# A hybrid SSD / attention / expert block: the four late modulation rows made in the projection stage instead of the attention stage

## The chip, the cores and the metric

One core of one Trainium2 chip runs the whole kernel in one launch. The metric is the device time of that launch in microseconds (us); the median of three runs is 2930.75 us (2930.63 to 2934.76).

## The reference, cut to what matters

One trunk layer over 1024 latent tokens of width 1024, all in float32:

```python
mod = jax.nn.silu(c) @ w_ada[l] + b_ada[l]                 # 1 x 6144
sh1, sc1, g1, sh2, sc2, g2 = [m[:, None, :] for m in jnp.split(mod, 6, axis=-1)]
h = modulate(layer_norm(x), sh1, sc1)
y, yc = token_mixer(h, hc, cos, sin, w_in[l], ...)         # projection, SSD scan, attention, gates, w_o
x = layer_norm_affine(DEEPNORM_ALPHA * x + g1 * y, ln1_g[l], ln1_b[l])
h = modulate(layer_norm(x), sh2, sc2)
x = layer_norm_affine(DEEPNORM_ALPHA * x + g2 * expert_choice_ffn(h, ...), ln2_g[l], ln2_b[l])
```

The first two rows of `mod` (sh1, sc1) are needed at the very start and are made there. The case is about the other four, g1, sh2, sc2 and g2: each is a product of the 1024 numbers silu(c) with a 1024 x 1024 part of `w_ada`, plus a part of `b_ada`. They are first used after the output projection `w_o`.

## The kernel before, in words

The program is a sequence of stages; each is a block in which every engine has its own instruction stream, and a block ends with all engines meeting. The stages are: front (norm, first modulation), projection of features (`project_f_stage`), projection of tokens with the state recurrence (`project_states_stage`), scan output, attention, branch, residual, experts, output.

**`project_f_stage`** makes 24 channel blocks of xBC, 10 of q and k, and 16 gate blocks, each of 128 output features by 1024 tokens. For one block SyncE loads 512 KB of `w_in` (L368), ScalarE and VectorE split it in a high and a low part (L447, L522), TensorE makes 48 matmuls (L386), and ScalarE takes the result out of PSUM (L479 for a gate, with a sigmoid). GpSimd stores the results: `store_split` (L599, L601) the q and k blocks, `store` (L593) the gates. TensorE goes through gates 2 to 15 in a hardware loop. While gates are made, the buffers `qk_hi`, `qk_lo`, `conv_acc` and `t_out`, and the PSUM bank `f_tp`, are unused. `Ahead` is the first weight slab of the next stage, loaded and split here (L511, L569).

**`attention_stage`** goes through 8 query blocks of 128 tokens. A table of tiles sets the order: 20 tiles for a middle query block, each with a score product (L1498), an exponential (L1549) and a product with the values (L1510); row maxima for the next block (L1482, L1579) lie between. SyncE does the small transfers between engines for every block: `gather_sums` (L1418), `spread_inverse` (L1423, then a wait, then L1428), `load_top` (L1406 to L1410), and the query loads (L1395 to L1397). Beside this GpSimd makes the four modulation rows. `w_ada` is split so that partition p holds rows 8p to 8p+7, so a row needs 8 parts of [128, 1024] (512 KB each), 32 in all:

```python
pool.dma_start(ada_w[:, j % RING], wa[:, k, (2 + c) * D:(3 + c) * D])          # L1653, load_part
G_.tensor_scalar(ada_w[..], ada_w[..], ada_cond[:, k:k + 1], None, ALU.mult)   # L1663, scale
G_.tensor_tensor(ada_sum[..], ada_sum[..], ada_w[..], ALU.add)                 # L1666, add
```

The sum over the 128 partitions is left undone there; each of the four [128, 1024] sums goes to DRAM as `mod_parts` (L1682).

**`residual_stage`** multiplies by `w_o`, which it loads in four slabs of 1 MB through two buffers (L1953) and splits (ScalarE L2120, VectorE L2206). Before its first product TensorE spreads seven rows over all partitions (`spread_row`, L2028 and L2030): the three plain rows b_o, ln1_g and ln1_b by a matmul that picks one of seven, and the four modulation rows by this and a matmul of `ones` with the 2 MB of `mod_parts` (L2117), which adds up the partitions. ScalarE keeps them (`keep_row`, L2109 and L2111) between its casts of the weight slabs, and stores g2 for the expert stage. TensorE's first product with `w_o` (L2001) needs all seven rows spread and all four slabs split.

Of the kernel before, what the change touches and what calls it, by code (L numbers as in the profile page):

```python
# [15 lines left out]
ALU = mybir.AluOpType  # L16
ACT = mybir.ActivationFunctionType
AX_X = mybir.AxisListType.X
F32 = mybir.dt.float32
# [4 lines left out]
P = 128  # L24
D = 1024
KT = D // P
# [274 lines left out]
def project_f_stage(s, hi, lo, ahead, xbcF, xbcT, qkH, qkL, gF):  # L301
# [7 lines left out]
    with ExitStack() as st:  # L309
# [12 lines left out]
        tap = own(st, nc, "conv_tap_cols", [P, 2, CONV_W + 1])  # L322
        lat = bank(st, nc, "f_lat", [P, 2, SEQ])
# [12 lines left out]
        ctx_turned = s.sem("f_ctx_turned")  # L336
        rot_step = s.sem("f_rot_step")
# [7 lines left out]
        NF = NX + NQK + NG  # L345

# [9 lines left out]
        with nc.Block() as block:  # L356

            @block.sync
            def _(sp):
# [4 lines left out]
                for col, f0, n in ((XBC0, 0, NX), (Q0, NX, NQK), (G0, NX + NQK, NG)):  # L364
                    with sp.Fori(0, n // 2) as i:
                        for b in range(2):
                            sp.wait_ge(w_free, 2 * i + (f0 + b + 1))
                            sp.dma_start(w[:, b], wv[:, :, ds(2 * P * i + (col + P * b), P)]).then_inc(w_in[b], 16)  # L368
                ahead.load(s, sp)

            @block.tensor
            def _(pe):
# [60 lines left out]
                with pe.Fori(1, NG // 2) as i:  # L433
                    for b in range(2):
                        product(2 * i + (NX + NQK + b), b, False)

            @block.scalar
            def _(act):
# [16 lines left out]
                def evacuate(f, b, kind, turn, within):  # L455
# [20 lines left out]
                    else:  # L476
                        act.wait_ge(qk_lo_made, NQK - 1 + b)
                        act.wait_ge(wide_out[b], 16 * turn - 16 * NQK // 2)
# [36 lines left out]
            def _(dve):  # L515
# [49 lines left out]
                with dve.Fori(1, NG // 2) as i:  # L565
                    split_lo(2 * i + (NX + NQK), 0)
                    split_lo(2 * i + (NX + NQK + 1), 1)
                dve.wait_ge(ahead.hi_made, 1)
                nc.vector.tensor_tensor(ahead.lo[:], ahead.raw[:], ahead.hi[:].bitcast(F32), ALU.subtract).then_inc(ahead.split, 1)  # L569

            @block.gpsimd
            def _(pool):
# [9 lines left out]
                def store(f, b, kind, turn, within):  # L582
                    row = within * P
                    rows = slice(row, row + P) if isinstance(row, int) else ds(row, P)
                    if kind == "xbc":
                        pool.wait_ge(wide_made, f + 3)
                        pool.dma_start(xbcF[rows, :], wide[:, b]).then_inc(wide_out[b], 16)
                        pool.wait_ge(tp_free, f + 2)
                        pool.dma_start(xbcT[:, rows].rearrange("(c p) n -> p c n", p=P),
                                       turned[:, b].rearrange("p (c n) -> p c n", n=P)).then_inc(turned_out[b], 16)  # L590
                    else:
                        pool.wait_ge(acc_free, f + 3)
# [2163 lines left out]
```

## Time and profile before

| what | value |
| --- | --- |
| median of 3 runs | 2930.75 us |
| the profiled execution: its own time, and its span from first to last instruction | 2933.16 us, 2931.5 us |
| TensorE busy / GpSimd busy over the span | 2504.5 us (85%) / 705.8 us (24%) |
| granted TensorE clock, mean | 0.915 of full |
| gates in `project_f_stage` | from about 628 to 797 us |
| attention stage | from about 1314 to 1680 us |
| residual stage | from 2047.9 us, first product with `w_o` at 2103.6 us |

A profile row tells for a group of instructions the line, engine, operation, output<-input by the program's names, the count, the busy time and the mean of one, and the idle time of the engine before them with what ended it. PE is TensorE, DVE VectorE, ACT ScalarE, POOL GpSimd, SP SyncE; PEld is TensorE's weight load, and a q behind an engine's name its instruction queue. Times of a row in the timeline are start and duration in us.

### The profile page before, as it was taken

To read this page: it belongs to the slowest core of one execution; us is meant where nothing else is said; L and a number is where in the kernel's file an instruction comes from. 1 tells how busy PE (TensorE), PEld (TensorE's weight loads), DVE (VectorE), ACT (ScalarE), POOL (GpSimd) and SP (SyncE) were. 2 spreads that over 40 slices of the span, in tenths; PEclk is the share of its full clock that TensorE was granted. 3 is DMA by queue.
4 is the path that set the end of the run, shared out by engine and by line. 5 is a ranking of instruction groups with operands and counts; after the bars stand their busy time and mean duration, and the time that the engine had idled before them with its cause. 6 is when DMAs were issued, how large, how long until landed. Compare 5 with 4: busy or idle time off the path is not lost. (4 is left out here: it accounts for less than half of the span.)

```text
span 2931.5 us, 31293 instructions
## 1 busy us (share of the span) xinstructions
PE 2504.5 (85%) x11848; PEld 1972.9 (67%) x11848; DVE 1597.0 (54%) x1674; ACT 1061.7 (36%) x1349; POOL 705.8 (24%) x487
## 2 busy tenths in 40 slices
PE   6799999999898996975989659698885499999992
PEld 2588888778697885653656448576474388888881
DVE  4455554431143665763556352532254699999994
ACT  3333333121131113541334341310232377777772
POOL 0001000010002434994992000000042212222113
PEclk8799999999999998996999869899697699999996
DMA  4333333342225867949564255543333599999994
GB/s 188 97 109 116 117 117 108 115 144 86 89 88 197 299 241 247 308 164 202 148 157 88 54 167 150 161 118 94 119 115 113 222 375 397 391 395 398 398 362 143
DMA packets 307553, 556.80 MB, mean 190 GB/s; under 512 B 22121, under 2 KB 212025, under 8 KB 283953
## 3 DMA queue, kind: packets, MB, share of 16 engines
q1 hardware_dynamic: 277938, 431.61, 43.3%
q0 software_dynamic: 27200, 115.10, 12.1%
q10 hardware_dynamic: 2304, 8.62, 0.8%
q8 instruction: 68, 1.11, 0.2%
q14 instruction: 43, 0.35, 0.0%
HBM read 434.22 MB, written 120.79 MB: 189 GB/s over the span
## 5 line engine op out<-in xcount | busy, mean ns | idle before, releaser
L2412 DVE TENSOR_TENSOR e_wlo<-e_w,e_whi 128x2048 fp32r<-128x2048 f32 x188 | 425.7, 2290 | 43.5 <-ACT e_whi L2365 42.2
L2365 ACT CAST e_whi<-e_w 128x2048 fp32r<-128x2048 f32 x192 | 366.3, 1915 | 120.8 <-PE e_gu L2525 83.5
L386 PE MATMUL f_lat<-h_hi,w_hi 128*128 128x512 f32 x800 | 254.4, 399 | 0.3 <-DVE w_lo L522 0.3
L386 PE MATMUL f_lat<-h_lo,w_hi 128*128 128x512 f32 x800 | 250.7, 394 | 0.0
L386 PE MATMUL f_lat<-h_hi,w_lo 128*128 128x512 f32 x800 | 250.6, 394 | 0.0
L522 DVE TENSOR_TENSOR w_lo<-w_raw,w_hi 128x1024 fp32r<-128x1024 f32 x50 | 61.3, 1225 | 216.9 <-ACT w_hi L447 216.9
L1889 PE MATMUL b_acc<-b_hi,b_whi 128*128 128x512 f32 x384 | 151.4, 394 | 14.0 <-DVE b_lo L1840 14.0
L1579 DVE CUSTOM_DVE_ANT_0 a_masked<-a_a_ps,a_mask 128x640 f32<-128x640 f32 x128 | 105.5, 825 | 99.3 <-PE a_a_ps L1483 95.9
L1510 PE MATMUL a_c_ps<-a_prob,a_v 128*128 128x512 f32 x304 | 157.8, 602 | 0.0
L386 PEld LDWEIGHTS f_lat<-h_hi,w_hi 128*128 128x128 f32 x800 | 136.0, 188 | 30.5 <-issue 4.8
L386 PEld LDWEIGHTS f_lat<-h_hi,w_lo 128*128 128x128 f32 x800 | 136.0, 188 | 27.7
L386 PEld LDWEIGHTS f_lat<-h_lo,w_hi 128*128 128x128 f32 x800 | 136.0, 188 | 27.5
L1549 ACT ACTIVATE a_prob<-a_b_ps 128x512 f32<-128x512 f32 x152 | 89.5, 597 | 177.4 <-DVE a_b_ps L1597 84.5
L535 DVE SCALAR_TENSOR_TENSOR conv_acc<-conv_in,conv_tap_cols,conv_acc 128x1284 f32<-128x1284 f32 x96 | 149.4, 1556 | 3.4
L1889 PE MATMUL b_acc<-b_lo,b_whi 128*128 128x512 f32 x384 | 151.1, 393 | 0.0
L1889 PE MATMUL b_acc<-b_hi,b_wlo 128*128 128x512 f32 x384 | 150.7, 393 | 0.0
L2525 PE MATMUL e_gu<-e_whi,e_xhi 128*128 128x512 f32 x512 | 140.4, 396 | 3.9 <-DVE e_xlo L2416 2.4
L2525 PE MATMUL e_gu<-e_wlo,e_xhi 128*128 128x512 f32 x512 | 138.6, 393 | 0.0
L2525 PE MATMUL e_gu<-e_whi,e_xlo 128*128 128x512 f32 x512 | 138.6, 393 | 0.0
L1498 PE MATMUL a_b_ps<-a_q,a_k 128*128 128x512 f32 x152 | 120.9, 796 | 18.9 <-ACT a_prob L1549 10.7
L2589 POOL DMA_INDIRECT moe<-e_y,e_scatter_rows x16 | 44.6, 2785 | 378.0 <-DVE e_y L2433 378.0
L1482 PE MATMUL a_a_ps<-a_k,a_q 128*128 128x256 f32 (+1 forms) x256 | 80.8, 335 | 44.5 <-DMA a_q<-qkH 41.1
(346 smaller groups left out, 5627.8 us busy)
## 6 DMA issues: line engine op xcount, KB each, us to landing
e_w<-in_w_gate_up SPq DMA_DIRECT2D x128, 1024.0 KB, 10.4
e_w<-in_w_down SPq DMA_DIRECT2D x64, 1024.0 KB, 8.7
w_raw<-in_w_in SPq DMA_DIRECT2D x50, 512.0 KB, 4.0
t_space<-xbcT POOLq DMA_DIRECT2D x18, 1280.0 KB, 6.4
before<-t_space SPq DMA_DIRECT2D x16, 1024.0 KB, 4.2
y_before<-before SPq DMA_DIRECT2D x64, 256.0 KB, 6.1
a_ada_w<-in_w_ada POOLq DMA_DIRECT2D x32, 512.0 KB, 4.1
b_w<-in_w_ssd_br SPq DMA_DIRECT2D x16, 1024.0 KB, 5.6
```

Of the source, the lines that this page charges most:

```text
L386: mm = nc.tensor.matmul(o, weights[:, b, k, :], part[:, k, a:a + n], start=(k == 0 and n_pass == 0), stop=(k == KT - 1 and n_pass == 2))
L522: nc.vector.tensor_tensor(wlo[:, b], w[:, b], whi[:, b].bitcast(F32), ALU.subtract).then_inc(w_free, 1)
L535: nc.vector.scalar_tensor_tensor(conv[:, b], padded[:, b, c:c + W_OUT], tap[:, b, c:c + 1], conv[:, b], ALU.mult, ALU.add).then_inc(conv_s ...
L1482: nc.tensor.matmul(a_ps[:, h % 2, out], q1[:, j, h], k1[:, g, keys], start=True, stop=False)
L1498: nc.tensor.matmul(b_ps[:, T % 2], k1[:, g, keys], q1[:, n % QB, heads], start=True, stop=False)
L1510: nc.tensor.matmul(out, values(v, c, g), prob[:, T % PR], start=first, stop=last).then_inc(tiles_summed, 1)
L1549: nc.scalar.activation(prob[:, T % PR], b_ps[:, T % 2], ACT.Exp, scale=SCALE).then_inc(exps_made, 1)
L1579: V.tensor_tensor_reduce(masked[:, h % 2], a_ps[:, h % 2, A0:A0 + KEYS], mask[:, variant(m)], 1.0, NEG, ALU.add, ALU.max, top[:, h:h + 1]) ...
L1889: mm = nc.tensor.matmul(acc[:, b, j], weights[:, b, k, :], xpart[:, k, :], start=(k == ks[0] and n_pass == 0), stop=(k == ks[-1] and n_pas ...
L2365: nc.scalar.copy(whi[:, slot % SPLIT], w[:, slot]).then_inc(w_hi, 1)
L2412: V.tensor_tensor(wlo[:, slot % SPLIT], w[:, slot], whi[:, slot % SPLIT].bitcast(F32), ALU.subtract).then_inc(w_split, 1)
L2525: mm = nc.tensor.matmul(gu[:, 512 * c:512 * c + 512], part[:, b, k, :], weights[:, slot % SPLIT, 512 * c:512 * c + 512], start=(k == 0 and ...
```

## The change

The four rows are made in `project_f_stage`, by GpSimd, while TensorE makes the gates. The 32 parts go the same way (load, scale, add), now with 8 adds for each row onto a sum that is cleared first and holds the bias in partition 0. TensorE sums the 128 partitions by a matmul with a column of ones: rows 0, 1 and 2 after gates 5, 9 and 13, and row 3 after the last gate. VectorE copies a row out of PSUM, and SyncE stores it to `mod`. GpSimd's gate stores go to SyncE, on the queue of the weight loads, and the gate loops are written out. In the attention stage nothing is left of this work. In the residual stage the seven spread rows are gone: six rows are loaded from DRAM with a broadcast over the partitions, by ScalarE behind its first cast, and the `mF` tile 1 is loaded before slab 2. The core of the diff:

```diff
 def project_f_stage
+        ada_w = (qhi[:, 0, 0:D].bitcast(F32), qhi[:, 1, 0:D].bitcast(F32), qlo[:, 0, 0:D].bitcast(F32))
+        ada_sum, ada_row = (conv[:, 0, 0:D], conv[:, 1, 0:D]), turned[0:1, 0, 0:D]
+        SUM_AFTER = {5: 0, 9: 1, 13: 2}
@@ sync
+                for n in range(NG):
+                    sp.wait_ge(w_free, NX + NQK + n + 1)
+                    sp.dma_start(w[:, n % 2], wv[:, :, G0 + P * n:G0 + P * n + P]).then_inc(w_in[n % 2], 16)
+                    if n >= 3:
+                        store_gate(n - 3)
+                    if n - 2 in SUM_AFTER:
+                        store_rest(SUM_AFTER[n - 2])
                 ahead.load(s, sp)
...
@@ tensor
-                with pe.Fori(1, NG // 2) as i:
-                    for b in range(2):
-                        product(2 * i + (NX + NQK + b), b, False)
+                def sum_rest(c):
+                    pe.wait_ge(ada_step, KT * c + KT)
...
+                    for half in range(2):
+                        mm = nc.tensor.matmul(tp[0:1, 512 * half:512 * half + 512], ones[:], ada_sum[c % 2][:, 512 * half:512 * half + 512], start=True, stop=True)
+                    mm.then_inc(ada_summed, 1)
+                for n in range(2, NG):
+                    product(NX + NQK + n, n % 2, False)
+                    if n in SUM_AFTER:
+                        sum_rest(SUM_AFTER[n])
+                sum_rest(REST - 1)
@@ vector
+                def keep_row(c):
+                    dve.wait_ge(ada_summed, c + 1)
+                    if c:
+                        dve.wait_ge(ada_out, 16 * c)
+                    nc.vector.tensor_copy(ada_row, tp[0:1, :]).then_inc(ada_made, 1)
...
@@ gpsimd
-                pairs(pool, "gate", store)
+                def load_part(j):
+                    c, k = divmod(j, KT)
+                    if j >= 3:
+                        pool.wait_ge(ada_step, j - 2)
+                    pool.dma_start(ada_w[j % 3], wa[:, k, (2 + c) * D:(3 + c) * D]).then_inc(ada_in[j % 3], 16)
...
+                for b in range(2):
+                    pool.wait_ge(qk_out[b], 16 * (NQK + NQK - NQ))
+                    pool.wait_ge(turned_out[b], 16 * NX // 2 + 16)
+                pool.wait_ge(rot_step, 2 * NQK)
+                pool.wait_ge(cond_in, 16)
+                clear_sum(0)
+                for j in range(2):
+                    load_part(j)
+                for j in range(PARTS):
+                    if j + 2 < PARTS:
+                        load_part(j + 2)
+                    if j % KT == 4 and j // KT + 1 < REST:
+                        clear_sum(j // KT + 1)
+                    add_part(j)
+                pool.wait_ge(ada_out, 16 * REST)
 def attention_stage
...
-                for j in range(PARTS):
-                    if j + RING - 1 < PARTS:
-                        load_part(j + RING - 1)
-                    add_part(j)
...
 def residual_stage
@@ sync
                 load_w(1)
+                load_m(1)
                 for n in range(2, 4):
                     sp.wait_ge(w_split, n - 1)
                     load_w(n)
-                load_m(1)
@@ tensor
-                for j in range(len(ROWS)):
-                    spread_row(j)
                 pe.wait_ge(w_split, 4)
@@ scalar
-                    if n >= 1:
-                        keep_row(2 * n - 2)
-                        keep_row(2 * n - 1)
+                    if n == 0:
+                        for j, row in ((G1, mod[0:1, 2 * D:3 * D]), (B_O, s.x["b_o"]), (LN_G, s.x["ln1_g"]), (LN_B, s.x["ln1_b"]),
+                                       (SC2, mod[0:1, 4 * D:5 * D]), (SH2, mod[0:1, 3 * D:4 * D])):
+                            act.dma_start(rowv[:, j], row.to_broadcast([P, D])).then_inc(rows_in, 16)
```

How GpSimd's stream stands behind the last q and k store (`qk_lo`) in `project_f_stage`; before, the gate stores alone, in a loop:

```order
L601 DMA qkL<-qk_lo 128x256
L352 UNCONDITIONAL_BRANCH
L352 ISA
L593 ISA
L593 DMA gF<-f_out 128x1024
L592 REGISTER_ALU
L593 ISA
L593 DMA gF<-f_out 128x1024
L352 REGISTER_ALU
L352 COMPARE_AND_BRANCH
L593 DMA gF<-f_out 128x1024 x2
L356 UNCONDITIONAL_BRANCH
```

and now (the parts of `w_ada` lie in `qk_hi` and `qk_lo`, the sum in `conv_acc`):

```order
L660 DMA qkL<-qk_lo 128x256
L675 MEMSET conv_acc 128x1024
L677 DMA conv_acc<-in_b_ada 1x16x64
L670 DMA qk_hi<-in_w_ada 128x1024 x2
L670 DMA qk_lo<-in_w_ada 128x1024
L682 ISA
L682 TENSOR_SCALAR qk_hi<-qk_hi,f_cond 128x1024
L687 TENSOR_TENSOR conv_acc<-conv_acc,qk_hi 128x1024
L670 DMA qk_hi<-in_w_ada 128x1024
L682 TENSOR_SCALAR qk_hi<-qk_hi,f_cond 128x1024
L687 TENSOR_TENSOR conv_acc<-conv_acc,qk_hi 128x1024
```

The last three rows repeat to the 32nd part, with a clear and a bias load before parts 4, 12 and 20; no gate store is left there.

TensorE's stream at the end of the gates and into the next stage (`t_acc`), now:

```order
L421 MATMUL f_lat<-h_lo,w_hi 128x512 x2
L421 MATMUL f_lat<-h_hi,w_lo 128x512 x2
L477 MATMUL f_tp<-conv_acc,f_ones 1x512 x2
L367 UNCONDITIONAL_BRANCH
L869 UNCONDITIONAL_BRANCH
L877 MATMUL t_acc<-t_w_first_hi,h_hi 128x320
```

The L477 row is new; it stands between the last gate and the branch out of the block, and likewise behind gates 5, 9 and 13.

ScalarE's stream from the start of the residual stage to its last weight cast, now:

```order
L2134 CAST r_whi<-r_w 128x8x256
L2138 DMA r_rows<-mod 128x1024
L2138 DMA r_rows<-in_b_o 128x1024
L2138 DMA r_rows<-in_ln_g 128x1024
L2138 DMA r_rows<-in_ln_b 128x1024
L2138 DMA r_rows<-mod 128x1024 x2
L2092 CAST r_mhi<-r_m 128x1024
L2134 CAST r_whi<-r_w 128x8x256
L2092 CAST r_mhi<-r_m 128x1024
L2134 CAST r_whi<-r_w 128x8x256 x2
```

Before, six copies of spread rows (L2111) stood between these casts, two behind each of the last three, and a seventh (L2109) behind them.

## Rows read from the trace of the kernel before

**Rows 1.** The page: the head, and the group of VectorE's weight splits.
```profile
span 2931.5 us, 31293 instructions
...
L522 DVE TENSOR_TENSOR w_lo<-w_raw,w_hi 128x1024 fp32r<-128x1024 f32 x50 | 61.3, 1225 | 216.9 <-ACT w_hi L447 216.9
```

**Rows 2.** Timeline, gates and the start of the next stage: start, duration, what [idle before].
```profile
640.81 0.55 POOL L601 DMA_DIRECT2D qkL<-qk_lo  x1
...
786.10 1.02 ACT L479 ACTIVATE f_out<-f_lat 128x1024 f32<-128x1024 f32 x1 [9.24 <-PE f_lat L386]
...
797.30 1.02 ACT L479 ACTIVATE f_out<-f_lat 128x1024 f32<-128x1024 f32 x1 [7.96 <-PE f_lat L386]
798.62 0.53 POOL L593 DMA_DIRECT2D gF<-f_out  x1 [10.67 <-ACT f_out L479]
...
806.15 0.31 POOL L970 MEMSET t_zeros<- 128x256 f32 x1 [6.99 <-POOLq L356]
```

**Rows 3.** Timeline of GpSimd in the attention stage, one part and the next one's start.
```profile
1428.74 2.85 POOL L1663 TENSOR_SCALAR a_ada_w<-a_ada_w,a_ada_cond 128x1024 f32<-128x1024 f32 x1
1431.67 2.35 POOL L1666 TENSOR_TENSOR a_ada_sum<-a_ada_sum,a_ada_w 128x1024 f32<-128x1024 f32 x1
1434.32 0.59 POOL L1653 DMA_DIRECT2D a_ada_w<-in_w_ada  x1 [0.30 <-POOL a_ada_sum L1666]
1434.96 2.84 POOL L1663 TENSOR_SCALAR a_ada_w<-a_ada_w,a_ada_cond 128x1024 f32<-128x1024 f32 x1
```

**Rows 4.** Timeline of SyncE's queue, attention: the same step of blocks 0, 3, 4.
```profile
1414.21 0.56 SPq L1418 DMA_DIRECT2D a_sums<-a_cols  x1
...
1539.61 0.54 SPq L1418 DMA_DIRECT2D a_sums<-a_cols  x1
...
1575.51 0.55 SPq L1418 DMA_DIRECT2D a_sums<-a_cols  x1
```

**Rows 5.** Windows, attention: us, PE PEld DVE ACT POOL busy, clock, DMA share, GB/s.
```profile
1355.00:1375.00 20.00, 6.44 (x20) 4.77 (x20) 4.17 (x10) 0.00 (x0) 11.91 (x10) 0.60 1.05 226
1400.00:1555.00 155.00, 143.42 (x560) 96.30 (x559) 89.93 (x181) 54.69 (x98) 143.71 (x76) 0.96 0.62 157
1555.00:1655.00 100.00, 100.00 (x379) 64.92 (x378) 53.91 (x116) 44.21 (x80) 0.35 (x1) 1.00 0.26 55
```

**Rows 6.** Timeline of TensorE at the start of attention.
```profile
1362.83 0.58 PE L1482 MATMUL a_a_ps<-a_k,a_q 128*128 128x256 f32 x1 [9.72 <-DMA a_q<-qkH]
...
1377.49 0.80 PE L1498 MATMUL a_b_ps<-a_q,a_k 128*128 128x512 f32 x1 [8.14 <-DMA a_sunk_spread<-a_sunk]
```

**Rows 7.** Windows, start of the residual stage; columns as in rows 5.
```profile
2050.00:2066.00 16.00, 3.79 (x5) 1.73 (x6) 3.64 (x3) 4.84 (x4) 0.00 (x0) 0.50 1.02 354
```

**Rows 8.** Timeline at the start of the residual stage: ScalarE, TensorE, VectorE.
```profile
2053.61 1.90 ACT L2120 CAST r_whi<-r_w 128x2048 fp32r<-128x2048 f32 x1 [42.45 <-DMA r_w<-in_w_o]
...
2062.21 3.75 PE L2028 MATMUL r_row_ps<-r_base_rows,r_ident 7*128 7x512 f32 x4 [21.29 <-DMA r_parts<-mod_parts]
...
2092.58 2.29 DVE L2206 TENSOR_TENSOR r_wlo<-r_w,r_whi 128x2048 fp32r<-128x2048 f32 x1 [12.30 <-ACT r_whi L2120]
...
2103.56 1.84 PE L2001 MATMUL r_acc<-r_whi,r_mhi 128*128 128x512 f32 x2
```

**Rows 9.** DMA issues: count, KB each, median us from issue to landing.
```profile
qkL<-qk_lo POOLq DMA_DIRECT2D x2, 128.0 KB, 4.9
...
a_ada_w<-in_w_ada POOLq DMA_DIRECT2D x32, 512.0 KB, 4.1
```

**Rows 10.** Timeline, VectorE and GpSimd at once: states stage, then attention stage.
```profile
970.42 3.63 POOL L968 TENSOR_TENSOR t_space<-t_space,t_tab 128x2048 f32<-128x2048 f32 x1
...
971.85 4.37 DVE L898 TENSOR_TENSOR t_space<-t_space,t_tab 128x2048 f32<-128x2048 f32 x1
...
998.89 4.00 POOL L968 TENSOR_TENSOR t_space<-t_space,t_tab 128x2048 f32<-128x2048 f32 x1 [0.93 <-DMA t_space<-xbcT]
...
1437.15 0.67 DVE L1611 TENSOR_TENSOR a_cols<-a_cols,a_inverse 64x512 f32<-64x512 f32 x1
```

More of the change, by code:

```diff
@@ L336, in project_f_stage @@
         ctx_turned = s.sem("f_ctx_turned")
+        cond_in, ones_made, ada_in = s.sem("f_cond_in"), s.sem("f_ones_made"), [s.sem(f"f_ada_in{b}") for b in range(3)]
+        gate_out = [s.sem(f"f_gate_out{b}") for b in range(2)]
+        ada_blank, ada_bias_in = s.sem("f_ada_blank"), s.sem("f_ada_bias_in")
+        ada_scaled, ada_step, ada_summed, ada_made, ada_out = (s.sem(f"f_ada_{n}") for n in ("scaled", "step", "summed", "made", "out"))
         rot_step = s.sem("f_rot_step")
@@ L345, in project_f_stage @@
         NF = NX + NQK + NG
+        REST = 4
+        PARTS = REST * KT
+        SUM_AFTER = {5: 0, 9: 1, 13: 2}
+        wa = s.x["w_ada"][0].rearrange("(p k) n -> p k n", k=KT)
         def pairs(eng, kind, step):
@@ L1325, in attention_stage @@
         sums, inv_sums = own(st, nc, "a_sums", [P, QH]), own(st, nc, "a_inv_sums", [P, QH])
-        RING = 3
-        PARTS = 4 * KT
-        ada_cond, ada_w, ada_sum = own(st, nc, "a_ada_cond", [P, KT]), own(st, nc, "a_ada_w", [P, RING, D]), own(st, nc, "a_ada_sum", [P, 2, D])
-        cond_in, ada_in = s.sem("a_cond_in"), [s.sem(f"a_ada_in{b}") for b in range(RING)]
-        ada_scaled, ada_step, ada_out = s.sem("a_ada_scaled"), s.sem("a_ada_step"), [s.sem(f"a_ada_out{b}") for b in range(2)]
-        wa = s.x["w_ada"][0].rearrange("(p k) n -> p k n", k=KT)
         a_ps = bank(st, nc, "a_a_ps", [P, 2, 1024])
@@ L2102, in keep_turned @@
                     nc.scalar.copy(h2F[:], tp[:]).then_inc(cols_made, 1)
-                def keep_row(j):
-                    kind = ROWS[j][0]
-                    out = (row_ps[:], tp[:].rearrange("p k q -> p (k q)"))[j % 2]
-                    act.wait_ge(spread, j + 1)
-                    if kind is None:
-                        nc.scalar.copy(g2[:], out[0:1]).then_inc(rows_kept, 1)
-                    else:
-                        nc.scalar.copy(rowv[:, kind], out).then_inc(rows_kept, 1)
-                act.dma_start(ident[:], s.squares[:, 0:P]).then_inc(const_in, 16)
-                for j, (kind, part) in enumerate(ROWS):
-                    src = s.x["b_ada"][:, (2 + part) * D:(3 + part) * D] if part is not None else s.x[{B_O: "b_o", LN_G: "ln1_g", LN_B: "ln1_b"}[kind]]
-                    act.dma_start(base_rows[j:j + 1, :], src).then_inc(base_in, 16)
-                act.dma_start(parts[:], mod_parts).then_inc(parts_in, 16)
                 for n in range(4):
```

156 lines of the change are left out of this document (67 added, 89 removed).

## The prediction, made before the changed kernel ran

> **What bounds the kernel now.** I read the page first, for the busy share of each engine, and then the timeline of each of the three stages that the change touches, since each has a limit of its own. The chain that ended last covers only the output stage and says nothing here.
>
> In the gates TensorE is the bound. The sigmoid copies of two gates that follow each other start 11.20 us apart (786.10 and 797.30), and every gate from the second on keeps that pace; GpSimd only issues a store for each, and the next stage starts 7.5 us after the last store's issue [rows 2]. VectorE has one split of 1.2 us in each 11.2 us [rows 1]. So GpSimd has the time from 640.8 to about 797 us nearly free, some 156 us.
>
> The work that is to go there takes longer. In the attention stage one part costs GpSimd 6.22 us from scale to scale: 2.85 scale, 2.35 add, then 0.30 and 0.59 for the issue of the next load, and small gaps [rows 3]. GpSimd waits for hardly anything else there; it is a chain on one engine, and 32 parts make 199 us. **32 times 6.22 does not fit in 156.**
>
> In attention this work is off the chain of computing but not free. SyncE's step `gather_sums` comes once in a block of 20 tiles. Blocks 0 to 3 take 125.4 us for three (41.8 each) while the loads of `w_ada` run, and the next, after the last load, 35.9 us [rows 4]. The windows say the same: up to 1555 us TensorE is busy 143.4 of 155 us at clock 0.96 with the DMA engines at 0.62; after it, busy all the time at 1.00, DMA at 0.26 [rows 5]. The parts compete with the query loads and the small round trips on which a block's start hangs. At the start of the stage the DMA engines are full from 1355 to 1375 us (226 GB/s), and TensorE waits 9.7 us for queries and 8.1 us for a small transfer behind them [rows 5, 6].
>
> In the residual stage the first product starts at 2103.6 us, though the first slab was in at 2053.6 [rows 8]. Between them TensorE spreads seven rows at a granted clock of 0.50 [rows 7], after the 2 MB of `mod_parts` have landed at 2062.2, and ScalarE's row copies hold up its cast of the last slab, so that this slab's split starts only at 2092.6 [rows 8].
>
> **The change, part by part.**
>
> 1. *The rows in the gates.* GpSimd's last q/k store is issued at 640.8 and lands 4.9 us later [rows 2, 9]: 645.7. The clear of 1024 columns: 0.31 us for 256 [rows 2], so at most 1.2. Then 0.3 and 0.55 us until the bias load is issued, 4.1 us for the first part to land [rows 9] and 0.3 to start: 652.2. Thirty parts at 6.22: 838.8. The last two have no load to issue, 5.3 each: 849.4. Three more clears with their bias loads at 1.2 + 0.3 + 0.55 = 2.05: 855.6.
>
> TensorE cannot run ahead of this. After gate 5 (end about 685) it waits for part 8, due at 652.2 + 49.8 + 2.05 = 704, so 19 us; after gate 9 and gate 13 a few us each; gate 15 ends at about 832, and then it waits some 25 us for part 32. None of these waits adds to the end: GpSimd never waits for TensorE (the clears that need a sum come 20 us behind it), so the end is GpSimd's. What is queued behind the waiting TensorE, VectorE's split and row copy and SyncE's loads, is two gates ahead and has slack. I cost the moved gate stores, the written-out loops and the three inner sums (at most 3.75 us each) at nothing: GpSimd's chain covers them by some 25 us, and without that cover the sums would cost 8 to 11 us.
>
> Then the tail, which nothing covers: four matmul instructions at half clock, 3.75 us [rows 8], VectorE's copy of 1024 columns, half of the 2.29 us for 2048 [rows 8], and a store up to the next stage, for which I take the 7.5 us of the gate store. Together 12.4.
>
> 2. *Sharing with VectorE.* In the states stage a VectorE operation on two SBUF operands that starts inside one of GpSimd's takes 4.37 us; it ends 2.17 us after GpSimd's ends, which is its bare length. GpSimd's own went from 3.63 to 4.00 us beside such an operation [rows 10]. So each holds the other up. But a VectorE operation at 1437.15 took a bare 0.67 us inside GpSimd's scale of 1434.96 to 1437.80 [rows 3, 10]: the scale lets go long before its end. About 13 splits of 1.2 us fall in the chain. One that meets an add waits for its end and runs in the 0.9 us before the next scale, at 0.3 us for GpSimd; one in the first half of a scale costs nothing. I take 0.3 us each, 4 us in all, between 0 and 13 x 1.2 = 16.
>
> The Trainium skill ("SBUF — State Buffer", section "SBUF: two separate sides") speaks against this change: whichever of VectorE and GpSimd starts first has the shared pair of ports for its whole instruction, and the other is blocked. The states rows agree; the 0.67 us inside the scale does not. By the rule alone the sum would have 16 us here and not 4.
>
> So the stage ends at 855.6 + 4 + 12.4 = 872.0 and not at 806.15: **65.9 us later.**
>
> 3. *Attention without the parts.* Three blocks fall from 41.8 to 35.9 us: 17.7 us. At the start, four loads of 0.5 MB fall into the full queue, 2.1 MB, 9.3 us at 226 GB/s; TensorE's two waits there total 17.9 us. Not all of a queue's time is on the chain, so I take 6, between 0 and 9.3. **23.7 us earlier**, between 17.7 and 27. GpSimd's own time of 190 us that goes is worth nothing: it ended 100 us before the stage.
>
> 4. *Residual stage.* Seven spreads on TensorE, seven copies on ScalarE and 2 MB go; six broadcasts of 512 KB come. The first product now waits for the last slab alone. Bytes until it is in: 4 MB of weights, 1 MB of `mF`, 3 MB of rows, 8.4 million bytes; at the 354 GB/s from 2050 on [rows 7], that is 23.7 us, then 1.90 cast and 2.29 split: 2077.9. **25.7 us earlier** than 2103.6. With the 226 GB/s of the attention start it would be 37.2 us of loading, and 12.2 earlier; with the row loads out of the way, 14.8 us of loading and 34.6 earlier. I take 354, the rate of the same loads in the same place. The rows' own wait (VectorE before the first norm) is covered by the first product of 13 us.
>
> Sum: 65.9 - 23.7 - 25.7 = +16.5 us on a span of 2931.5: 2948.0. The profiled execution's own time is 1.7 above its span and 2.4 above the median of the runs, so against the median of 2930.75 this is **2947 us**.
>
> **The rivals.**
>
> *A. The port lock in full* (the rule above): every split in the chain costs GpSimd its 1.2 us, 16 and not 4. 2959 us. For it, the states rows; against it, the operation inside the scale. Chance 0.12.
>
> *B. The broadcasts crowd out the slabs.* The residual stage gains 12.2 us and not 25.7, as at 226 GB/s: 2961 us. For it, a queue of small pieces does run at that rate in attention; against it, the row loads here have long pieces of 4 KB. Chance 0.10.
>
> *C. The giving back is at its upper ends*, 27 and 34.6 us: +4.3, 2935 us, within what can be told from no change, about 0.2% or 5.9 us. For it, the start of attention is all transfers; against it, the slabs go through two buffers, each waiting for a split. Chance 0.14.
>
> *D. Faster: GpSimd's part is shorter here.* If the load's issue and its wait (0.9 us) fell out of the chain, because the queue now has this work alone, a part would take 5.3 us, the chain would be 28 us shorter and the 4 us of sharing gone too: 65.9 - 32 - 49.4 = -15, about 2915 us. It decides from 5.5 us a part down. Against it: the wait comes before every issue, full queue or not [rows 3], and the code's order of load, scale and add is the same. Chance 0.07.
>
> **How the numbers follow.** The forecast of 2947 has the remaining 0.57, between about 2939 and 2955. Slower by over 0.2%: the forecast, A and B, less a little, 0.77. Within 0.2%: nearly all of C and that little, 0.15. Faster: D and the edge of C, 0.08. The range from 2934 to 2962 takes in A, B and C alone; it leaves out D and A with B together.
>
> **What would show it.** The next stage starting near 872 us. GpSimd busy without a break from 646 to 858, at 6.2 us a part. TensorE waiting about 19 us for GpSimd after gate 5 and 25 us after the last gate. `gather_sums` 36 us apart in all middle blocks. In the residual stage, the first product some 30 us after the stage's start and not 56. I am wrong if GpSimd's part takes below 5.5 us, if TensorE has no wait after gate 5, or if the attention blocks stay above 40 us without the loads.

## The result, and the profile after

The changed kernel takes 2953.5 us (median of 4 runs, 2949.7 to 2956.7) beside 2932.8 for the kernel before in the same session: ratio 1.0068, 95% interval [1.0048, 1.0089]. A second comparison of the unaltered change, with more runs, gave 2951.1 beside 2934.0: 1.0064 [1.0051, 1.0076]. **It is 17 to 21 us slower.** The profiled execution of the change took 2949.7 us, the fastest of its four, with a span of 2948.2; that is 16.7 more than the span of 2931.5 before.

The timeline of GpSimd, VectorE, TensorE and SyncE in the changed kernel, at the start of the gates, at gate 5, at gate 9 and at the end of the stage (start us, duration us, engine, line, operation, out<-in; in brackets the idle time before and what ended it). The last row but one is the first instruction of the next stage and answers to the last one of [rows 2]:

```profile
641.07 0.55 POOL L660 DMA_DIRECT2D qkL<-qk_lo  x1
647.75 0.95 POOL L675 MEMSET conv_acc<- 128x1024 f32 x1 [6.13 <-issue]
653.73 2.85 POOL L682 TENSOR_SCALAR qk_hi<-qk_hi,f_cond 128x1024 f32<-128x1024 f32 x1 [2.62 <-DMA qk_hi<-in_w_ada]
656.66 2.39 POOL L687 TENSOR_TENSOR conv_acc<-conv_acc,qk_hi 128x1024 f32<-128x1024 f32 x1
659.35 0.60 POOL L670 DMA_DIRECT2D qk_hi<-in_w_ada  x1 [0.30 <-POOL conv_acc L687]
660.00 2.85 POOL L682 TENSOR_SCALAR qk_hi<-qk_hi,f_cond 128x1024 f32<-128x1024 f32 x1
...
704.55 3.17 PE L477 MATMUL f_tp<-conv_acc,f_ones 128*1 128x512 f32 x4 [19.09 <-POOL conv_acc L687]
...
761.63 1.21 DVE L623 COPY t_out<-f_tp 1x1024 f32<-1x1024 f32 x1 [15.07 <-PE f_tp L477]
761.83 4.39 POOL L687 TENSOR_TENSOR conv_acc<-conv_acc,qk_hi 128x1024 f32<-128x1024 f32 x1
762.77 1.20 DVE L575 TENSOR_TENSOR w_lo<-w_raw,w_hi 128x1024 fp32r<-128x1024 f32 x1
...
860.92 2.34 POOL L687 TENSOR_TENSOR conv_acc<-conv_acc,qk_hi 128x1024 f32<-128x1024 f32 x1
863.31 3.57 PE L477 MATMUL f_tp<-conv_acc,f_ones 128*1 128x512 f32 x4 [24.84 <-POOL conv_acc L687]
866.92 1.21 DVE L623 COPY t_out<-f_tp 1x1024 f32<-1x1024 f32 x1 [31.70 <-PE f_tp L477]
868.16 0.25 SPq L389 DMA_DIRECT2D mod<-t_out  x1
875.41 0.31 POOL L1066 MEMSET t_zeros<- 128x256 f32 x1 [12.15 <-POOLq L367]
```

The first part takes 6.27 us from scale to scale (653.73 to 660.00); the parts that nothing disturbs take 6.20 to 6.28. The chain takes 209.5 us from the first scale to the end of the last add at 863.3, and the next stage starts 12.15 us later, at 875.4. Before it was 806.15: 69.3 us. TensorE waited 19.1 us at its first sum and 24.8 at its last, and once the chain ran nothing held GpSimd up except VectorE's operations at the same time (the add of 4.39 us). The groups of GpSimd's operations over the whole chain (mean ns behind the busy time) give the sum of that: 174.6 us for 32 scales and 32 adds, which at their bare 2.85 and 2.34 would be 166.1, so 8.5 us of sharing (10.5 us in the trace of x11, the same kernel run again):

```profile
L682 POOL TENSOR_SCALAR qk_hi<-qk_hi,f_cond 128x1024 f32<-128x1024 f32 x22 | 64.4, 2926 | 3.5 <-DMA qk_hi<-in_w_ada 2.6
L687 POOL TENSOR_TENSOR conv_acc<-conv_acc,qk_hi 128x1024 f32<-128x1024 f32 x22 | 56.3, 2558 | 1.8
L682 POOL TENSOR_SCALAR qk_lo<-qk_lo,f_cond 128x1024 f32<-128x1024 f32 x10 | 28.5, 2854 | 0.4
L687 POOL TENSOR_TENSOR conv_acc<-conv_acc,qk_lo 128x1024 f32<-128x1024 f32 x10 | 25.4, 2540 | 0.8
```

From there two stages give back. In attention, `gather_sums` (L1508 now) of the blocks that took 41.8 us each [rows 4]:

```profile
1473.76 0.56 SPq L1508 DMA_DIRECT2D a_sums<-a_cols  x1
...
1509.81 0.55 SPq L1508 DMA_DIRECT2D a_sums<-a_cols  x1
...
1581.65 0.54 SPq L1508 DMA_DIRECT2D a_sums<-a_cols  x1
```

That is 36.0 us a block, 107.9 for three and not 125.4. In the residual stage the row copies are gone from ScalarE, and the splits of the four slabs (before, the last of them came at 2092.6 [rows 8]) are these, with the wait of TensorE behind them:

```profile
2096.25 2.29 DVE L2213 TENSOR_TENSOR r_wlo<-r_w,r_whi 128x2048 fp32r<-128x2048 f32 x1 [11.98 <-ACT r_whi L2134]
2101.02 2.29 DVE L2213 TENSOR_TENSOR r_wlo<-r_w,r_whi 128x2048 fp32r<-128x2048 f32 x1 [1.34 <-ACT r_whi L2134]
2114.87 2.29 DVE L2213 TENSOR_TENSOR r_wlo<-r_w,r_whi 128x2048 fp32r<-128x2048 f32 x1 [2.47 <-ACT r_whi L2134]
2117.86 2.29 DVE L2213 TENSOR_TENSOR r_wlo<-r_w,r_whi 128x2048 fp32r<-128x2048 f32 x1 [0.70 <-ACT r_whi L2134]
```
```profile
PE r_acc L2049 <- DVE r_wlo L2213: 38.0, 1, 38.0
```

The first product starts at 2120.2. The stage began at 2089.2, so 31.0 us after the start and not 55.6. The balance, each as the shift against the kernel before at the marks named: gates +69.3 (next stage's start, 806.1 to 875.4); states and scan +2.1 (attention's first matmul, 1332.2 to 1403.6, is 71.4 later); attention -29.5 (the branch stage's first transpose, 1692.5 to 1734.4, is 41.9 later); branch -0.6; residual -24.6 (first product 16.7 later). The rest moves by nothing: the span is 16.7 longer. This is the balance of one trace against one; how far single terms of it scatter is said below the next table.

### The profile page after: what moved, and what is told of

The parts are those of the page before. It is cut to its first block and busy times, and to the rows that moved or that the text cites. A ratio compares the mean times of both kernels' runs of the same rounds, so it can differ in the third digit from the quotient of the medians.

```text
span 2948.2 us, 31069 instructions
## 1 busy us (share of the span) xinstructions
PE 2468.5 (84%) x11820; PEld 1957.5 (66%) x11820; DVE 1598.5 (54%) x1678; ACT 1054.9 (36%) x1342; POOL 711.7 (24%) x478
```

## The experiments

All are compared with the kernel before in their own session; where a run is set against the change, the change's 2951.1 us of its longer comparison (x11) is used. Three marks are read from every trace: the start of the stage after the gates, the length of attention (first matmul on queries and keys to the branch stage's first transpose), and the time from the residual stage's first cast to its first product.

| run | median us | ratio to before [95%] | gates end | attention | residual |
|---|---|---|---|---|---|
| before | | | 806.1 | 360.4 | 50.0 |
| change | 2953.5 | 1.0068 [1.0048, 1.0089] | 875.4 | 330.9 | 25.9 |
| x1 gate stores alone | 2929.5 | 0.998 [0.997, 0.999] | 805.7 | 353.6 | 49.2 |
| x2 24 parts (work left out) | 2901.6 | 0.9885 [0.9864, 0.9906] | 825.9 | 330.4 | 26.1 |
| x3 16 parts (work left out) | 2891.1 | 0.9845 [0.9823, 0.9868] | 814.9 | 330.9 | 25.7 |
| x4 sums last | 2949.7 | 1.0046 [1.0029, 1.0063] | 874.0 | 330.9 | 26.0 |
| x5 loads in attention | 2966.7 | 1.0113 [1.0096, 1.0129] | 877.1 | 351.4 | 25.7 |
| x6 compute in attention | 2960.3 | 1.0094 [1.0077, 1.0110] | 878.3 | 336.8 | 25.8 |
| x7 parts on VectorE | 2891.4 | 0.9864 [0.9847, 0.9880] | 815.6 | 331.1 | 25.8 |
| x8 rows late | 2947.1 | 1.0044 [1.0030, 1.0058] | 880.3 | 332.4 | 18.9 |
| x9 = x7 + x8 | 2886.7 | 0.9837 [0.9819, 0.9855] | 816.8 | 331.3 | 18.8 |
| x10 splits twice | 2958.0 | 1.0076 [1.0056, 1.0096] | 888.4 | 331.1 | 25.7 |
| x11 change again | 2951.1 | 1.0064 [1.0051, 1.0076] | 878.0 | 331.0 | 25.6 |
| x12 both in attention | 2975.0 | 1.0144 [1.0129, 1.0158] | 878.2 | 355.5 | 25.5 |

How close a single trace may be read shows where several have the same code. The gates of the change stand in six traces (change, x5, x6, x8, x11, x12) and end at 875.4 to 880.3 us, the change's own being the earliest. Its attention stands in nine and takes 330.4 to 332.4. The attention of the kernel before stands in two, and takes 360.4 in its own trace and 353.6 in x1. The kernel before has medians of 2932.4 to 2935.2 in the sessions, so a difference of medians from two sessions is good to some 3 us.

### What sets the end of the gates

**x1**: the kernel before, with the gate loops written out and the stores on SyncE.

```diff
-                        pool.wait_ge(acc_free, f + 3)
-                        pool.dma_start(gF[rows, :], wide[:, b, CTX:TOK]).then_inc(wide_out[b], 16)
+                    sp.wait_ge(acc_free, f + 3)
+                    sp.dma_start(gF[row:row + P, :], wide[:, n % 2, CTX:TOK]).then_inc(gate_out[n % 2], 16)
```

> Only one part of the change is made: the gate loops written out and the gate stores issued by SyncE; the modulation rows stay in attention and the residual stage is the old one. Theory 1 (the added time is GpSimd's chain of 32 parts and nothing else in the gates): the gates end where they did, 806 us within 2 us, and the time is that of the kernel before, 2931 us, within 3 us. Rival (part of the 69 us comes from the stores behind SyncE's weight loads, or from the written-out loops): the gates end 5 us or more later, the time is 2936 us or more. A small gain of 3 to 5 us at the gates' end would also be possible, since the last store no longer goes through GpSimd.

Measured: the gates end at 805.7 us against 806.1, and the time is 0.1 to 0.3% under the kernel before. The stores and the loops cost nothing, as the prediction had them. The small gain is not in the gates; in this trace it lies in attention (353.6 us, with the same code there), and I do not know why. Its three blocks took 121.5 us where the trace before had 125.4:

```profile
1409.05 0.56 SPq L1431 DMA_DIRECT2D a_sums<-a_cols  x1
...
1530.56 0.54 SPq L1431 DMA_DIRECT2D a_sums<-a_cols  x1
```

So what the change gives back in attention is 22.7 to 29.5 us, by which of the two traces it is set against.

**x2** and **x3**: fewer parts, all else as in the change. Each of the four rows is summed from six, or four, of its eight parts, so these two kernels leave out work of the reference and are no versions of it; they serve as a measure alone.

```diff
+        NK = 6
-        PARTS = REST * KT
+        PARTS = REST * NK
```

> The change with 24 parts in place of 32: each row is summed from six of its eight parts, and the last two loads, scales and adds of each row are left out; sums, copies and stores stay. Theory 1 (GpSimd's chain sets the end of the gates): 8 parts of 6.27 us fall from the end, 50 us, and a microsecond or two of port sharing: the chain ends at about 812 us, the stage at about 824, the whole at 2901 us (2897 to 2906). Rival (TensorE's waits for sums and the clock that falls in them make the end): three inner sums and their waits stay, the end moves by less than 30 us and the time stays above 2920.

> The same with 16 parts, half of each row left out. The chain would end at about 762 us, before TensorE's last gate at 798. Theory 1: GpSimd no longer sets the end; TensorE does, with three inner sums of up to 3.75 us each on its path and the tail after the last gate (sum, copy, store), so the stage ends at 806 plus 8 to 15 us, 814 to 821, and the time is 2891 to 2899 us, only a few us under the run with 24 parts. Rival (every part costs its 6.27 us wherever it lies, for instance by crowding the weight loads): another 50 us less than with 24 parts, about 2850 us.

Measured: 8 parts fewer end the gates 49.5 us earlier (875.4 to 825.9), 6.2 us each, and the time falls by as much, to 2901.6. Sixteen fewer end them only 11.0 us earlier again, at 814.9. So down to some 22 parts (an estimate: 60.5 us of gain at 6.2 us each is about 10 parts) each costs its full length, and below that TensorE sets the end. The waits in the gates show the change of hands: in x3 it is GpSimd that waits for TensorE's sum to clear a sum buffer (first row), in the change TensorE for GpSimd (second row, all four sums; us in total, times, longest):

```profile
POOL conv_acc L676 <- PE f_tp L478: 13.5, 1, 13.5
```
```profile
PE f_tp L477 <- POOL conv_acc L687: 54.3, 4, 24.8
```

What is left is 814.9 against 806.1, 8.8 us. Each of the three inner sums lengthens its gate from 11.3 to 13.3 us (by the starts of the sigmoid copies), 6.1 us in all; the rest, 2.7 us, is put down to the last sum with its copy and store, and is within the scatter above.

**x4**: all four sums behind the last gate, from four buffers.

```diff
-        SUM_AFTER = {5: 0, 9: 1, 13: 2}
+        SUM_AFTER = {15: 0}
-                    if n in SUM_AFTER:
-                        sum_rest(SUM_AFTER[n])
-                sum_rest(REST - 1)
+                for c in range(REST):
+                    sum_rest(c)
```

> The change with all four column sums behind the last gate, from four separate sum buffers; the work is all there. TensorE then runs its 16 gates without waiting for GpSimd, and VectorE's splits come 11.2 us apart as before. Theory 1: GpSimd's chain is still the end, so it ends within 5 us of 863 us; behind it only the last sum, copy and store remain, the same 12 us: 2950 us within 5. Rival (the waits of TensorE on the inner sums cost the time, and the clock that falls meanwhile): the end of the gates comes back by 20 us or more, 2930 us or less.

Measured: TensorE now waits for GpSimd behind its last gate alone, 55.1 us in two pieces, the longer 44.3 (54.3 in the change, in four pieces), and the gates end at 874.0. Where it waits is without effect on the end; the rival falls.

**x10**: 14 more VectorE operations beside GpSimd's chain.

```diff
                 for n in range(2, NG):
+                    dve.wait_ge(hi_made, NX + NQK + n + 1)
+                    dve.wait_ge(extra, n - 2)
+                    nc.vector.tensor_tensor(padded[:, 0, 0:D], w[:, n % 2].rearrange("p k n -> p (k n)"), whi[:, n % 2].bitcast(F32).rearrange("p k n -> p (k n)"), ALU.subtract).then_inc(extra, 1)
                     split_lo(NX + NQK + n, n % 2)
```

> The changed kernel with 14 more VectorE operations in the gates: before each split the same subtraction of 1024 columns once more, into a buffer that nobody reads. It does no work of the reference, and TensorE doesn't need it. Theory 1 (GpSimd's chain lets most VectorE operations by, at 0.3 to 0.5 us each): the chain ends 4 to 7 us later than 863 us, 2955 to 2961 us. Rival A (the port is held in full for each): 14 times 1.2 us, 17 us later, 2967 us or more. Rival B (VectorE finds its gaps at no cost): 2951 us.

Measured by the groups of the chain in this trace:

```profile
L686 POOL TENSOR_SCALAR qk_hi<-qk_hi,f_cond 128x1024 f32<-128x1024 f32 x22 | 62.8, 2854 | 5.4 <-DMA qk_hi<-in_w_ada 4.5
L691 POOL TENSOR_TENSOR conv_acc<-conv_acc,qk_hi 128x1024 f32<-128x1024 f32 x22 | 61.3, 2785 | 1.8
L686 POOL TENSOR_SCALAR qk_lo<-qk_lo,f_cond 128x1024 f32<-128x1024 f32 x10 | 30.0, 2996 | 0.4
L691 POOL TENSOR_TENSOR conv_acc<-conv_acc,qk_lo 128x1024 f32<-128x1024 f32 x10 | 29.5, 2948 | 0.8
```

183.6 us, 9.0 more than in the change's first trace and 7.0 more than in its second (176.6): 0.5 to 0.64 us for each added operation, where the lock in full was priced at 1.2. The chain's end missed what Theory 1 expected: it ends at 876.2, 13 us later than the change's 863.3, and not 4 to 7. Of this, 4 us are a later start (the first scale at 657.7), which has nothing to do with the chain, and 9.0 are its sharing. The median, 2958.0, lies within what Theory 1 expected and under the 2967 of the full lock; whether the price is 0.5 or 0.64 it cannot tell.

### What attention gave back

**x5**: the 32 loads alone; **x6**: the scales and adds alone; **x12**: both, tied together as before.

```diff
+                for j in range(4 * KT):
+                    if j:
+                        pool.wait_ge(ada_in, 16 * j)
+                    pool.dma_start(ada_w[:, j % 3], wa[:, j % KT, (2 + j // KT) * D:(3 + j // KT) * D]).then_inc(ada_in, 16)
```
```diff
+                for j in range(4 * KT):
+                    if j:
+                        pool.wait_ge(ada_step, j)
+                    G_.tensor_scalar(ada_w[:, j % 3], ada_w[:, j % 3], 0.5, None, ALU.mult).then_inc(ada_scaled, 1)
+                    pool.wait_ge(ada_scaled, j + 1)
+                    G_.tensor_tensor(ada_sum[:], ada_sum[:], ada_w[:, j % 3], ALU.add).then_inc(ada_step, 1)
```

> The changed kernel, and in attention the 32 loads of w_ada (512 KB each) once more, one behind the other, into a buffer that nobody reads; no scale or add. They do no work of the reference. Theory 1 (attention gained because these transfers went): the blocks with loads go back to 40 to 42 us from 36, for as long as the loads run (32 at 5 to 6 us, 160 to 190 us, four blocks or so), and the start loses its gain too: 20 to 30 us slower than the change, 2970 to 2982 us. Rival (GpSimd's scale and add held VectorE up at the shared port): the blocks stay at 36 us, 2951 us within 4.

> The changed kernel, and in attention GpSimd's 32 scales and adds of 1024 columns once more, on a cleared buffer and without any load; they do no work of the reference. Theory 1 (it was the transfers): blocks at 36 to 37 us, 2951 us, at most 5 us more. Rival (port sharing): the blocks at 40 us or more while the chain of 32 x 5.2 us runs, 2965 us or more.

> The changed kernel, with both the 32 loads and the 32 scales and adds once more in attention, tied together as they were in the kernel before; they do no work of the reference. Loads alone made the attention stage 20.6 us longer in the trace, compute alone 6.0 us, and the kernel before is 29.5 us longer. If the two add up, with the residual stage as in the change: the stage 27 to 30 us longer, 2976 to 2982 us. If they hide behind each other, 20 us or less, 2971 us.

Measured: against the change, the loads alone cost 15.6 us in the medians (2966.7 - 2951.1), the compute alone 9.2, both together 23.9. In the traces attention grows by 20.5, 5.9 and 24.6 us. Neither theory had it whole: **the transfers are the larger part, between three fifths (by the medians) and three quarters (by the traces), and GpSimd's computing is the rest**, and the two nearly add up. Together they bring attention back to 355.5 us, between the two traces that have the old code (353.6 and 360.4). The medians expected for x5 (2970 and more) were missed by 3 us, for x6 (2956 at most) by 4, for x12 (2976 and more) by 1, and the stage in x12 grew by 24.6 us where 27 to 30 were expected.

Each has its own marks. With the loads, VectorE waits for the round trip of `inv_rows`, once in a block (an 8 KB store and a load of 512 KB that spreads it). These are its two transfers in x5 and then in the change, with the median us from issue to landing behind the size:

```profile
a_inverse<-inv_rows SPq DMA_DIRECT2D x3, 512.0 KB, 6.7
inv_rows<-a_inv_sums SPq DMA_DIRECT2D x3, 8.0 KB, 3.8
```
```profile
a_inverse<-inv_rows SPq DMA_DIRECT2D x4, 512.0 KB, 4.7
inv_rows<-a_inv_sums SPq DMA_DIRECT2D x4, 8.0 KB, 1.4
```

The round trip is 4.4 us longer beside the loads, and the blocks are 4.1 to 5.1 us longer; beside the computing (x6) it takes 1.4 and 4.9. TensorE's waits for ScalarE's exponentials from 1440 to 1600 us total 8.4 us in x5, 3.4 in x6 and none in the change. That these waits follow from the round trip was not traced step by step. With the computing, VectorE's short operations on SBUF operands grow. The groups and a wait, x5 first, then x6, then the change, all from 1400 (the wait from 1440) to 1600 us:

```profile
DVE a_cols L1704 <- DMA a_inverse<-inv_rows: 9.4, 3, 3.6
```
```profile
L1704 DVE TENSOR_TENSOR a_cols<-a_cols,a_inverse 64x512 f32<-64x512 f32 x12 | 7.9, 675 | 9.4 <-DMA a_inverse<-inv_rows 9.4
```
```profile
L1703 DVE TENSOR_TENSOR a_cols<-a_cols,a_inverse 64x512 f32<-64x512 f32 x12 | 14.2, 1199 | 1.4 <-DMA a_inverse<-inv_rows 1.4
L1694 DVE TENSOR_TENSOR a_sums<-a_sums,a_sunk_spread 128x16 f32<-128x16 f32 x4 | 7.7, 1928 | 0.0
```
```profile
L1701 DVE TENSOR_TENSOR a_cols<-a_cols,a_inverse 64x512 f32<-64x512 f32 x12 | 7.9, 674 | 0.1
L1692 DVE TENSOR_TENSOR a_sums<-a_sums,a_sunk_spread 128x16 f32<-128x16 f32 x4 | 0.7, 170 | 0.0
```

The division of columns takes 675 ns in the change and beside the loads, 1199 beside the computing; the sums' add 170 and 1928. The blocks of x6 are 37.3 to 38.2 us apart, those of x5 40.1 to 41.1, those of the change 36.0.

### What the residual stage gave back

**x8**: the six broadcasts behind ScalarE's last cast.

```diff
-                    if n == 0:
+                    if n == 3:
                         for j, row in ((G1, mod[0:1, 2 * D:3 * D]), (B_O, s.x["b_o"]), (LN_G, s.x["ln1_g"]), (LN_B, s.x["ln1_b"]),
```

> The changed kernel with the six row broadcasts of the residual stage issued after ScalarE's cast of the last slab and not after that of the first, so that the slabs have the queues for themselves. Theory 1: the 3 MB of rows stood in the way of the slabs (9 us at 340 GB/s), so the first product comes 7 to 10 us earlier; of this some goes back, since the rows then land behind the first product of 13 us and the first norm waits: 2943 to 2951 us. Rival (the slabs are paced by their two buffers, cast and split, not by the queue): the first product at the same time, and the late rows cost 5 us or more: 2956 us.

Measured: from the first cast to the first product 18.9 us and not 25.9. So the broadcasts had crowded the slabs by 7.0 us, which is what Theory 1 gives. VectorE now waits 9.9 us for a row, and some of the gain goes there: 4.0 us of it reach the median (2947.1 against 2951.1, from two sessions, whose intervals against the kernel before overlap). The same edit took 4.7 us from x7 (x9 below), so its sign can be trusted more than its size.

```profile
DVE r_rows L2218 <- DMA r_rows<-mod: 9.9, 1, 9.9
```

### A version that beats both

**x7**: the parts on VectorE, in one operation each; GpSimd only issues the loads, into four buffers, and the sums come after gates 5, 8, 11 and 14. **x9**: the same with the late rows.

```diff
-                    nc.gpsimd.tensor_scalar(ada_w[j % 3], ada_w[j % 3], cond[:, k:k + 1], None, ALU.mult).then_inc(ada_scaled, 1)
-                    pool.wait_ge(ada_scaled, j + 1)
-                    nc.gpsimd.tensor_tensor(ada_sum[c % 2], ada_sum[c % 2], ada_w[j % 3], ALU.add).then_inc(ada_step, 1)
+                    nc.vector.scalar_tensor_tensor(ada_sum[c % 2], ada_w[j % 4], cond[:, k:k + 1], ada_sum[c % 2], ALU.mult, ALU.add).then_inc(ada_step, 1)
...
                     split_lo(NX + NQK + n, n % 2)
+                    for j in range(added, added + PARTS_AT.get(n, 0)):
+                        add_part(j)
```

> A version of the change in which the 32 parts are VectorE's: one operation each that multiplies and adds (1024 columns, some 1.2 to 1.5 us), three or two behind each of the splits 3 to 14, with GpSimd left to issue the loads; the sums stand after gates 5, 8, 11 and 14, so none is behind the last gate. Theory 1 (the change lost on the engine that carries the chain, not on the place): VectorE has 1.2 us of work in 11.2 us there, and 4 us more fit, so TensorE sets the end again: 806 us plus four sums of up to 3.75 us and nothing in the tail, 808 to 821 us. With attention and residual as in the change: 54 to 67 us less than the change, 2883 to 2896 us, faster than both kernels. Rival (VectorE's operations or the loads hold up the splits, so the gates lengthen to over 14 us each): 2930 us or more.

> The version with the parts on VectorE, and the six row broadcasts issued after ScalarE's last cast of a slab. Theory 1 (the two edits lie in different stages and add up): 2891 us of the one, less the 4 to 6 us that the late rows gave: 2885 to 2888 us, 1.5% under the kernel before. Rival (the rows then hold up the first norm as much as they had held up the slabs): 2891 us or more.

Measured: 2891.4 us for x7 and 2886.7 for x9, 0.9864 [0.9847, 0.9880] and 0.9837 [0.9819, 0.9855] of the kernel before. VectorE's groups in the gates of x7 (640 to 815 us):

```profile
L632 DVE SCALAR_TENSOR_TENSOR conv_acc<-qk_hi,f_cond,conv_acc 128x1024 f32<-128x1024 f32 x16 | 20.5, 1284 | 14.0 <-DMA qk_hi<-in_w_ada 12.9
L632 DVE SCALAR_TENSOR_TENSOR conv_acc<-qk_lo,f_cond,conv_acc 128x1024 f32<-128x1024 f32 x16 | 20.5, 1280 | 3.5 <-DMA qk_lo<-in_w_ada 2.9
L575 DVE TENSOR_TENSOR w_lo<-w_raw,w_hi 128x1024 fp32r<-128x1024 f32 x14 | 17.1, 1220 | 49.9 <-ACT w_hi L496 49.9
```

A part is 1.28 us there, where GpSimd needed 5.2 without the issue; all 32 together take 41 us of an engine that has 17 us of splits in these 175. The splits keep their bare 1.22, and the gates end at 815.6, where x3, with half of the parts on GpSimd, had 814.9. The unaltered change (**x11**) was run for reference:

> The changed kernel again, unaltered, so that the other runs have it with the same care as the kernel before: 2951 us within 3, ratio 1.005 to 1.008.

Measured: 2951.1 us, 1.0064 [1.0051, 1.0076], as expected.

## Why the prediction was right, and where it was not

The forecast, 2947 us and slower, holds in sign and size, and in its main cause: 16.5 us were predicted on the span and 16.7 came; in the medians it was 17 to 21, where 16 were predicted. But the closeness to 0.2 us is luck. The sharing was put 4.5 us too low and attention's gain, in this pair of traces, 5.8 us too low, and the two errors largely cancel. Besides, the end of the gates alone scatters by 5 us between traces of the same code, and this trace has the earliest.

*Step 1, the chain in the gates.* Right in cause (x2, x3, x4) and close in size: undisturbed parts of 6.20 to 6.28 us, where 6.22 was taken, first scale 1.5 us late, tail 12.15 and not 12.4. TensorE's waits were foreseen at 19 and 25 us and are 19.1 and 24.8. The stage ends 3.4 us later than the 872.0 predicted: 4.5 more for step 2, 1.5 for the late start, 0.25 less for the tail, and 2.3 less for the rest of the chain (a clear with its bias load took some 1.8 us and not 2.05). In the five other traces of these gates it is 5 to 8 us later than predicted. The claim that stores, loops and inner sums hide behind GpSimd holds: x1 shows it for the stores and loops, x4 for the place of the sums. The sums without that cover were put at 8 to 11 us; the gates of x3 and x7 end 8.8 and 9.5 us later than before, with all four.

*Step 2, sharing with VectorE.* Mis-sized: 8.5 us (10.5 in x11), where 4 were taken and 16 was the upper bound. The step looked at VectorE's operations that start inside one of GpSimd's, and let each of 13 splits cost 0.3 us. These cost GpSimd next to nothing. The price is paid the other way round, by operations of GpSimd that start while one of VectorE's runs: three adds that start beside the row copy behind a sum, with a split directly after it (the one of 4.39 us at 761.83; 5.8 us for the three), a scale that starts inside the larger split of the next stage's weights (1.6 us), and in x11 two adds that start 0.2 us into a split:

```profile
723.13 1.22 DVE L575 TENSOR_TENSOR w_lo<-w_raw,w_hi 128x1024 fp32r<-128x1024 f32 x1 [12.18 <-ACT w_hi L496]
723.34 3.27 POOL L687 TENSOR_TENSOR conv_acc<-conv_acc,qk_hi 128x1024 f32<-128x1024 f32 x1
```

The rows of the prediction had such a case and it was misread. GpSimd's operation of 4.00 us at 998.89 [rows 10] started inside one of VectorE's that ran from 997.12 for 2.29 us; the one of 3.63 us, taken there as undisturbed, had VectorE's begin inside it. The bare length of VectorE's operation is 2.29 us in that stage and not the 2.17 given, so it was let in 3.5 us into GpSimd's 3.63. The row of the kernel before that shows both:

```profile
997.12 2.29 DVE L898 TENSOR_TENSOR t_space<-t_space,t_tab 128x2048 f32<-128x2048 f32 x1 [6.82 <-DMA before<-t_space]
```

Rival A's price, 1.2 us for every split, is excluded by x10, though the measured 8.5 to 10.5 us lie about midway between its 16 and the 4 that were taken.

*States and scan.* Nothing was predicted, and 2.1 us came. From the gates' end to attention's first matmul all the traces, with the same code there, take 524.4 to 528.7 us, so this is within the scatter.

*Step 3, attention.* This step failed in one sentence: "GpSimd's own time of 190 us that goes is worth nothing". It was argued from GpSimd ending 100 us before the stage, which says only that nobody waits for its result. x6 shows that its operations beside VectorE's cost attention 5.9 us in the trace, and 9.2 in the medians. The step had 23.7 us, at most 27. Against the trace before 29.5 came: 17.5 from the three blocks (17.7 predicted, from the same rows) and 12 from the start and the first block, where at most 9.3 were allowed. Against x1's trace, with the same old code, 22.7 came, 13.6 of it from the three blocks and 9.1 from the rest. So the sentence is refuted, while whether the step's bound of 27 was passed stays open. From 1475 to 1583 us TensorE is now busy all the time at a granted clock of 1.00, with the DMA engines at 0.37, where it had 0.96 and 0.62 from 1400 to 1555 [rows 5].

*Step 4, the residual stage.* 24.6 us, where 25.7 were predicted, at 350 GB/s from 2090 to 2106 us and 326 from there to 2120, where 354 was taken. Rival B, the broadcasts in the way of the slabs, is right as a mechanism: x8 shows 7.0 us of it. They were counted in the 8.4 million bytes, so the forecast already held it; only the rival's low rate was wrong.

*Rival C*, attention and residual both at their upper ends, did not come: the residual stage gave 24.6 us and not 34.6. *Rival D* is excluded: a part did not get shorter on a queue of its own.

## What to carry to other kernels

Before work moves under another engine's shadow, multiply its length on the engine that carries it and compare with the shadow: 32 parts of 6.2 us did not fit in 156, and what stuck out was paid in full. The same work in the same place fitted when the engine with the cheaper operation took it, 1.28 us against 5.2. And an engine that "ends early" is not free: its transfers and its port are shared, and both can be priced apart by putting each back alone.

## What the hardware showed beyond that

The Trainium skill ("SBUF — State Buffer", section "SBUF: two separate sides") says that, where VectorE has two SBUF inputs and GpSimd reads SBUF, whichever starts first gets the shared pair of ports for its whole instruction and the other fully blocks. The traces here nearly agree for GpSimd's add of two SBUF operands, and not for its scale. Two pairs of rows of the run with 24 parts (x2), a split that starts 0.14 us into a scale and one that starts 0.55 us into an add:

```profile
655.93 2.86 POOL L683 TENSOR_SCALAR qk_hi<-qk_hi,f_cond 128x1024 f32<-128x1024 f32 x1 [2.72 <-DMA qk_hi<-in_w_ada]
656.07 2.06 DVE L576 TENSOR_TENSOR w_lo<-w_raw,w_hi 128x1024 fp32r<-128x1024 f32 x1 [10.53 <-ACT w_hi L497]
```
```profile
780.60 2.40 POOL L688 TENSOR_TENSOR conv_acc<-conv_acc,qk_hi 128x1024 f32<-128x1024 f32 x1
781.15 2.93 DVE L576 TENSOR_TENSOR w_lo<-w_raw,w_hi 128x1024 fp32r<-128x1024 f32 x1 [9.62 <-ACT w_hi L497]
```

The bare split is 1.22 us. The first ends at 658.13, so it was let in 0.98 us after the scale's start, though the scale is shown with 2.86 us. The second was let in at 782.86, 2.26 us into an add of 2.40. In x2, x4 and x10 six splits that start from 0.1 us before to 0.6 us into a scale take 1.6 to 2.3 us, all let in at 0.98 to 1.00 us, and eleven that start later than 0.9 us take their bare 1.2 to 1.3. So a scale that comes first keeps VectorE out for its first microsecond, an add for nearly all of its length. Where both start together either can win: in x4 a split that starts 0.03 us after a scale (654.91) took its bare 1.23, and the scale 3.90. The same page of the Trainium skill (section "Who interferes with whom") says that GpSimd contends where it reads and not where it only writes; a split beside GpSimd's clear of 1024 columns (732.36 us in the change, clear from 732.08) took 1.23, so the trace agrees.

The other way round both kinds of GpSimd's operations wait for a split that is already running (the add of 3.27 us above; a scale of 4.47 at 833.47). The row pair at 761.63 to 763.97 above is odd in one point: the add starts 0.2 us into the copy and 0.9 us before the split, and still it is the split that runs at its bare 1.20 and the add that ends 2.3 us behind it. The copy alone doesn't hold it: in x4 an add of 818.12 us took its bare 2.34 beside a copy that had begun at 817.78. Why a split that waits behind a copy comes before the add stays open.

The Trainium skill ("GPSIMD Engine Reference", section "Engine selection") puts GpSimd at about half of VectorE's speed for two operands and at about line rate for one. Here the add of two operands took 2.34 us beside 1.22 for VectorE's split of the same size, so that agrees. The scale of one operand took 2.85, longer than the add; VectorE's one-operand operation on the same 1024 columns in the residual stage, which adds a constant, took 0.68, so that does not:

```profile
2120.07 0.68 DVE L2218 TENSOR_SCALAR r_rows<-r_rows 128x1024 f32<-128x1024 f32 x1
```
